# Token-major w_in slices in wider pairs, MLA rotation on GpSimd, and new orders for both mixer stages

## The reference

```
z = rms_norm(h, norm1_g[l]) @ w_in[l]
y = concat([mlstm_mixer(...), mla_mixer(...), gla_mixer(...), conformer_conv(...)])
h = h + group_rms_norm(y, fuse_g[l], 4) @ w_out[l]
u = rms_norm(h, norm2_g[l])
h = h + (swiglu(u, ...) if l == 0 else moe_ffn(u, ...))    # 8 experts, top 2
```

## Time and profile before

| | |
|---|---|
| median of 3 runs | 1340.87 us (1340.64 to 1342.02) |
| the profiled execution's own time | 1339.72 us |
| its span | 1337.5 us |
| TensorE busy | 1259.0 us, 94% of the span |
| VectorE, ScalarE, GpSimd busy | 996.6, 832.9 and 145.0 us |
| mixers of layer 0, from the first transpose to those of the second norm | 17.4 to 154.5 us |
| mixers of layer 1, likewise | 359.7 to 499.1 us |
| mean granted clock of TensorE | 0.972 of full speed |

### The profile page before, as it was taken

One profiled execution on the slowest core, in us unless ns is written; L12 is line 12 of the kernel. 1 busy time (PEld: TensorE's weight loads), 2 busy tenths in 40 slices (PEclk: granted clock), 3 DMA queues, 4 the chain that ended last, 5 costly groups with the idle time before them and its releaser, 6 DMA issues.

```text
span 1337.5 us, 17758 instructions
## 1 busy us (share of the span) xinstructions
PE 1259.0 (94%) x6283; PEld 1053.5 (79%) x6283; DVE 996.6 (75%) x974; ACT 832.9 (62%) x825; POOL 145.0 (11%) x165
## 2 busy tenths in 40 slices
PE   4989899999798986899999999999999999999996
PEld 3889678888697975688888888888888888888885
DVE  4784444444558545888989989989889888988986
ACT  5557534444544744667777677777767767767774
POOL 4647000000045710000000000000000000000000
PEclk9989899999999996999999999999999999999998
DMA  9420685552333048799999999999999999999951
GB/s 292 127 98 8 253 313 189 184 183 75 94 96 126 2 152 304 284 348 331 354 359 341 357 350 340 363 343 349 362 338 358 358 338 357 357 340 354 360 205 49
DMA packets 175056, 347.41 MB, mean 260 GB/s; under 512 B 13166, under 2 KB 54272, under 8 KB 175008
## 3 DMA queue, kind: packets, MB, share of 16 engines
q1 hardware_dynamic: 173744, 344.43, 72.7%
q0 software_dynamic: 1232, 2.33, 0.8%
q10 hardware_dynamic: 32, 0.01, 0.0%
HBM read 345.68 MB, written 1.05 MB: 259 GB/s over the span
## 4 chain that ended last, share of the span: by engine, by line
PE 89%; DVE 6%; ACT 2%; DMA 2%; issue 0%; SPq 0%; DVEq 0%; ACTq 0%
PE bank L1583 15%; PE bank L1585 15%; PE bank L1584 15%; PE bank L1601 8%; PE bank L1600 8%; PE bank L1602 8%; PE bank L1553 3%; PE bank L1554 3%; PE bank L1555 3%; PE bank L1609 2%; PE bank L1943 1%; DVE low L970 1%; DVE uTl L988 1%; PE bank L1529 1%; PE bank L1728 1%; DMA ring<-in_w_in_dram 1%
## 5 line engine op out<-in xcount | busy, mean ns | idle before, releaser
L970 DVE TENSOR_TENSOR low<-ring,high 128x2048 fp32r<-128x2048 f32 x305 | 692.2, 2285 | 149.0 <-ACT high L613 146.8
L613 ACT ACTIVATE high<-ring 128x2048 fp32r<-128x2048 f32 x327 | 624.3, 1912 | 235.6 <-PE bank L1585 151.0
L1583 PE MATMUL bank<-high,uTh 128*128 128x512 f32 x880 | 350.7, 399 | 9.1 <-DVE uTl L988 3.3
L1585 PE MATMUL bank<-high,uTl 128*128 128x512 f32 x880 | 345.9, 393 | 0.0
L1584 PE MATMUL bank<-low,uTh 128*128 128x512 f32 x880 | 345.3, 392 | 0.0
L1583 PEld LDWEIGHTS bank<-high,uTh 128*128 128x128 f32 x880 | 166.8, 189 | 47.1 <-issue 7.1
L1585 PEld LDWEIGHTS bank<-high,uTl 128*128 128x128 f32 x880 | 166.7, 189 | 35.9
L1584 PEld LDWEIGHTS bank<-low,uTh 128*128 128x128 f32 x880 | 167.0, 190 | 32.7
L1601 PE MATMUL bank<-low,moe_hTh 128*128 128x512 f32 x352 | 140.1, 398 | 0.0
L1600 PE MATMUL bank<-high,moe_hTh 128*128 128x512 f32 x352 | 139.3, 396 | 0.0
L1602 PE MATMUL bank<-high,moe_hTl 128*128 128x512 f32 x352 | 138.5, 394 | 0.0
(11 more groups left out here) (370 smaller groups left out, 1483.0 us busy)
## 6 DMA issues: line engine op xcount, KB each, us to landing
ring<-in_moe_w_up_dram SPq DMA_DIRECT2D x176, 512.0 KB, 5.3
ring<-in_moe_w_gate_dram SPq DMA_DIRECT2D x176, 512.0 KB, 5.5
ring<-in_moe_w_down_dram SPq DMA_DIRECT2D x176, 512.0 KB, 5.2
ring<-in_w_in_dram SPq DMA_DIRECT2D x36, 512.0 KB, 4.8
ring<-in_ffn_w_up_dram SPq DMA_DIRECT2D x22, 512.0 KB, 5.2
ring<-in_ffn_w_gate_dram SPq DMA_DIRECT2D x22, 512.0 KB, 7.8
ring<-in_ffn_w_down_dram SPq DMA_DIRECT2D x22, 512.0 KB, 4.1
ring<-in_w_out_dram SPq DMA_DIRECT2D x16, 512.0 KB, 3.7
```

The source lines that it names most:

```text
L613: act.activation(high[:, n % SPLIT, 0:width], slot(n)[:, 0:width], ACT.Copy).then_inc(s["high_ready"], 1)
L970: dve.tensor_tensor(low[:, n % SPLIT, 0:width], slot(n)[:, 0:width], high[:, n % SPLIT, 0:width].bitcast(F32), ALU.subtract).then_inc(s["l ...
L1583: pe.matmul(o, ah, bh, start=(kd == 0), stop=False)
L1585: last = pe.matmul(o, al, bh, start=False, stop=(kd == KD - 1))
```

## The change

The 11 pieces of `w_in` are cut anew. Gates, both latents, the rotary key and the GLA's a (376 columns) are one token-major slice that comes first, as two pieces l0 and l1 of five and three feature blocks. The GLA's v and r (512 columns) become rg0 and rg1, the mLSTM's v and o (512 columns) become vo0 and vo1. Each pair fills one bank of PSUM for each token tile. Three streams of 48 matmuls, 376 or 512 columns wide, thus stand in the place of six of 176 to 256. The first half of l0 waits for each group of `uTl` apart. The rotation is done by GpSimd in eight operations. Two absolute values are taken by ScalarE instead of three small VectorE steps each, VectorE's min and subtract become one step, the four small `gref` steps and `negm` go to ScalarE, and the exponential of minus m is made from a TensorE sum. The rest is order: the small chains of gates and latents come before the convolution on VectorE, `fuse_transposes` 2 and 3 stand at other places among the halves of the output product, and banks are given out anew.

```diff
 W_IN_PIECES = {
-    "b": [(2424, 256)],
-    "a": [(2168, 256)],
-    "kv": [(1224, 160), (2152, 16)],
-    "if": [(1024, 200)],
-    "gqk": [(1384, 256)],
-    "mq": [(0, 256)],
-    "mk": [(256, 256)],
-    "v": [(512, 256)],
-    "o": [(768, 256)],
-    "r": [(1896, 256)],
-    "gv": [(1640, 256)],
+    "l0": ([(1024, 360), (2152, 16)], 0, 5),
+    "l1": ([(1024, 360), (2152, 16)], 5, 8),
+    "b": ([(2424, 256)], 0, 8),
+    "a": ([(2168, 256)], 0, 8),
+    "mq": ([(0, 256)], 0, 8),
+    "mk": ([(256, 256)], 0, 8),
+    "gqk": ([(1384, 256)], 0, 8),
+    "rg0": ([(1640, 512)], 0, 4),
+    "rg1": ([(1640, 512)], 4, 8),
+    "vo0": ([(512, 512)], 0, 4),
+    "vo1": ([(512, 512)], 4, 8),
 }
...
-        FUSE_BANKS = (2, 2, 4, 2)
+        FUSE_BANKS = (5, 0, 0, 0)
...
@@ gpsimd
-                split_low("if")
-                split_low("gqk")
+                split_low("a")
                 split_low("mq")
                 split_low("mk")
...
+                pool.wait_ge(s["kv_out"], l + 1)
+                pool.wait_ge(s["q_out"], l + 1)
...
+                for i, (a, b) in enumerate(((x1, cos), (x2, sin), (x2, cos), (x1, sin))):
+                    chain.done(pool.tensor_tensor(rt[:, i, :, :, :], a, b, ALU.mult))
+                chain.wait()
+                for i, op in ((0, ALU.subtract), (1, ALU.add)):
+                    out_ = slice(64 + 16 * i, 80 + 16 * i)
+                    pool.tensor_tensor(qtok[:, :, :, out_], rt[:, 2 * i, :, 0:4, :], rt[:, 2 * i + 1, :, 0:4, :], op)
+                    last = pool.tensor_tensor(ktok[:, :, :, out_], bc(rt[:, 2 * i, :, 4:5, :], [P, TT, HEADS, 16]),
+                                              bc(rt[:, 2 * i + 1, :, 4:5, :], [P, TT, HEADS, 16]), op)
+                last.then_inc(s["rot_ready"], 1)
...
@@ scalar
+                split_in("vo0")
                 for hd in range(HEADS):
...
                 last.then_inc(s["p_ready"], 1)
-                split_in("gv")
...
@@ tensor
-                pe.wait_ge(s["utl_ready"], 4 * (3 * l + 1))
...
+                        b = PAIR_BANKS[name[:-1]][i]
+                        if k0 == 0:
+                            claim(b, *reader)
+                        for k in range(k0, k1):
+                            if name == "l0" and i == 0 and k % 2 == 0:
+                                pe.wait_ge(s["utl_ready"], 4 * 3 * l + k // 2 + 1)
...
                 out_half(0, 1)
+                out_half(1, 0)
                 fuse_transposes(l, 2)
-                out_half(1, 0)
                 out_half(1, 1)
+                fuse_transposes(l, 3)
                 out_half(2, 0)
-                fuse_transposes(l, 3)
                 out_half(2, 1)
```

More of the change, by code:

```diff
@@ L57, with in_columns, in_width @@
 FEATURE_MAJOR = ("b", "a", "gqk", "mq", "mk")
+PAIR_ENDS = ("l1", "rg1", "vo1")
+def in_columns(name):
+    return sum(w for _, w in W_IN_PIECES[name][0])
+def in_width(name):
+    _, k0, k1 = W_IN_PIECES[name]
+    return (k1 - k0) * in_columns(name)
 POOL_LOWS = (3, 14)
@@ L1145, in gla_gates @@
[L1145 to L1153 removed]
+                dve.wait_ge(s["zl_ready"], 2 * (l + 1))
@@ L1207, in _ @@
-                for t in range(TT):
-                    dve.tensor_copy(qtok[:, t, :, 64:96], rot[:, t, 0:4, :])
-                    last = dve.tensor_copy(ktok[:, t, :, 64:96], bc(rot[:, t, 4:5, :], [P, HEADS, 32]))
-                last.then_inc(s["rot_ready"], 1)
-                dve.wait_ge(s["mcol_tr"], l + 1)
-                dve.tensor_copy(mcol[:, :], bank[0][:, 0:16]).then_inc(s["mcol_ready"], 1)
-                conv_steps(14, 16)
+                conv_steps(0, 8)
+                qk_conv("mq", 0, "qconv_ready")
@@ new lines, in _ @@
+                last.then_inc(s["ckv_tr"], 1)
+                half("b", 1)
+                pe.wait_ge(s["ckv_ready"], l + 1)
+                pe.wait_ge(s["ukv_in"], 64 * (l + 1))
+                claim(7, "gx_ready", l + 1)
+                pe.matmul(bank[7][:, 0:S], walpha[:, :], aT[:, :], start=True, stop=True).then_inc(s["gpre_ready"], 1)
+                pe.wait_ge(s["lf_ready"], l + 1)
+                claim(3, "mcum_ready", l + 1)
+                for t in range(TT):
+                    pe.transpose(bank[3][0:4, t * P:(t + 1) * P], gb[:, t, 0:4], ident[:, :])
+                    last = pe.transpose(bank[3][0:4, S + t * P:S + (t + 1) * P], gb[:, t, 4:8], ident[:, :])
@@ L1740, in _ @@
-                piece("if", "zif_ready")
-                pe.wait_ge(s["zkv_ready"], l + 1)
-                claim(7, "ckv_ready", l + 1)
-                for t in range(TT):
-                    pe.transpose(bank[7][:, t * P:(t + 1) * P], zkv[:, t, 0:P], ident[:, :])
-                    last = pe.transpose(bank[7][0:16, S + t * P:S + (t + 1) * P], zkv[:, t, 160:176], ident[:, :])
-                last.then_inc(s["ckv_tr"], 1)
-                half("gqk", 0, "gqk_ready")
-                pe.wait_ge(s["zif_ready"], l + 1)
@@ L1761, in _ @@
-                pe.matmul(bank[5][:, 0:S], walpha[:, :], aT[:, :], start=True, stop=True).then_inc(s["gpre_ready"], 1)
-                for t in range(TT):
-                    b = (7, 0)[t]
+                for t, b in enumerate(KV_BANKS):
                     claim(b, "kv_out", l + 1)
@@ L1843, in _ @@
                 last.then_inc(s["pv_ready"], 1)
+                pe.wait_ge(s["conv_done"], l + 1)
+                claim(4, "conf_n", l + 1)
+                for t in range(TT):
+                    for c in range(2):
+                        last = pe.transpose(bank[4][:, t * 256 + c * P:t * 256 + (c + 1) * P],
+                                            cacc[:, c, t * P:(t + 1) * P], ident[:, :])
+                last.then_inc(s["conf_tr"], 1)
+                piece("vo1")
+                pe.wait_ge(s["gla_qk"], l + 1)
@@ new lines, in _ @@
+                pe.wait_ge(s["gv_ready"], l + 1)
+                claim(2, "y_g", l + 1)
+                for t in range(TT):
+                    for hd in range(HEADS):
+                        o = bank[2][:, t * 256 + hd * DH:t * 256 + (hd + 1) * DH]
+                        v = gv[:, :, hd * DH:(hd + 1) * DH]
+                        if t == 0:
+                            last = pe.matmul(o, gS[:, hd, 0, :], v[:, 0, :], start=True, stop=True)
+                        else:
+                            pe.matmul(o, gS[:, hd, 1, :], v[:, 0, :], start=True, stop=False)
+                            last = pe.matmul(o, gS[:, hd, 2, :], v[:, 1, :], start=False, stop=True)
```

468 lines of the change are left out of this document (220 added, 248 removed).

## The result

The changed kernel takes 1304.20 us (median of 4 runs, 1299.99 to 1307.55); the kernel before, on the same chip, 1341.03 (4 runs, 1340.64 to 1342.02). The ratio is 0.9723, with a 95% interval of 0.9685 to 0.9761. A second set on another occasion gave 1305.17 against 1340.36, ratio 0.9733 (0.9719 to 0.9748). The profiled execution took 1299.99 us, the fastest of the four, with a span of 1298.0.

The account below looks back on a forecast made before the run. TensorE, busy 94% of the span, was taken as the bound, so gains lay in its time and gaps. Layer 0's 17.1 us and layer 1's 15.7 sum to 32.8: 1308.1 for a median, range 1301 to 1314, 1300 to 1320 with late cases.

Parts of the forecast that it names:

- five signs: No `ktok`/`qtok` wait; 376-column starts every 0.16-0.18 us; `uTl` wait at most 1; rotation 3-5; last fuse transposes at 103-107.
- Wider products: Token-major `w_in` matmuls: 2.55 us less for gates and latents, 1.2 for v, o, r and gv; 3.75 a layer.
- The rotation: Rotated keys in mid mk: GpSimd takes 4.0 us, ready 3.2 early; wait 4.8 and lower clock go, 6.7 a layer.
- vacated VectorE time: VectorE time freed by moving the rotation: costs and gains nothing by itself, since TensorE did not wait for the convolution.
- First group of `uTl`: Each layer's start: TensorE begins after two of eight `uTl` steps, 2.4 us earlier, idle time about 0.6 us.
- the clock behind it: Lower clock after the `uTl` wait costs 1.3 us in all; half its removal counted, 0.65 a layer.
- Start of layer 0: VectorE's copy of the gains stands behind fewer low-part columns: 1.0 us gained, between 0 and 2; nothing in layer 1.
- Output product: End of mixer part: last fuse transposes one half step earlier, 2.7 us a layer; 0.4 more in layer 0.
- New waits: Second fuse transposes wait for bank 0, 0.3 to 0.6 us; with others of that kind, 0.5 lost a layer.
- the rival in ScalarE's queue: vo0's high part amid the softmax's exponentials delays the probabilities' transposes: 5 us a layer, 1318; chance 0.14.
- the late rotation: GpSimd operations of 1.31 us each make TensorE wait 3.3 us, plus lower clock: 5.2 a layer, 1318; chance 0.13.
- the slow GpSimd: Strided, broadcast rotation operands many times slower on GpSimd: at 3.2 us each about 1346, slower than before; chance 0.03.

Follow-up runs that it names:

- second profile: The changed kernel run again unedited, its profiled execution at 1305.92 us with a span of 1304.1.
- e2_narrow: Changed kernel with each 376-column matmul issued as 200 and 176, each 512 as two of 256: median 1320.34 us, profiled execution 1311.55.
- e5_before_rot_pool: Kernel before, with only the rotation moved from VectorE to GpSimd, between the low parts of mk and v: 1326.50 us, ratio 0.9904.
- e6_rot_vector: Changed kernel with the rotation's same eight operations back on VectorE, before piece mq's convolution: 1306.40 us, ratio 0.9745.
- e4_all_groups: Changed kernel with the first l0 matmul waiting again for all four groups of `uTl`: 1310.62 us, ratio 0.9776.
- five variants: Five edited versions of the changed kernel that leave its wait for the first `uTl` group as it is; medians 1301.77 to 1314.13 us.
- e9_cols_early: Changed kernel with VectorE's first copy of the gains ahead of layer 0's normalization, not behind the low parts of l0 and l1: 1301.77 us, ratio 0.9710.
- e3_tail: Changed kernel with the last fuse transposes put back behind one more half of the output product: 1310.10 us, ratio 0.9766.
- e10_h_first: Changed kernel with h added before the first feed-forward piece's low part, and fewer bank claims before layer 0's feed-forward: 1304.26 us, ratio 0.9736.

## Why the prediction held, step by step

1308.1 us was forecast, 1304.2 and 1305.2 are the medians of the two sets: a gain of 32.8 us forecast and of 35.2 to 36.8 measured. All five signs named for "right" are there: no wait for `ktok` or `qtok`, 376 columns every 0.173 us, `uTl` waits of 0.8 and 0.9, a rotation of 3.8, and 103.9 us from the first l0 matmul to the last fuse transposes in both layers of the first profile. The mechanism is right, but the total is closer than its parts, as three stretches show (gain in us, against the kernel before):

| stretch | forecast | first profile | second profile |
|---|---|---|---|
| layer 0, to the first `w_in` matmul | 3.4 | 3.6 | 3.6 |
| layer 0, from there to the last fuse transposes | 13.3 | 15.2 | 14.7 |
| layer 0, from there to h's transposes | 0.4 | -0.1 | -1.6 |
| layer 1, transposes to the first `w_in` matmul | 2.4 | 2.3 | 2.3 |
| layer 1, from there to the last fuse transposes | 13.3 | 14.7 | 13.2 |
| layer 1, from there to h's transposes | 0 | 2.5 | 2.6 |

The long stretches gained up to 1.9 us more than their terms. The last ones missed both ways, and in layer 0 two errors cancel: that its sum came so near is luck. The parts:

- **Layer 0**: 17.1 us forecast, 16.6 and 18.7 in the two profiles. **Layer 1**: 15.7 forecast, 18.1 and 19.5. Most of what the sum missed lies in layer 1.
- **Wider products**, 3.75 a layer. The guessed 0.170 us for 376 columns is 0.173 (9 starts). The Trainium skill (TensorE: Matmul & The Clock Gate, section "Wait — 56ns, not 53.3ns?") gives an estimate of 159 ns there, and the trace does not agree, as at 512. Undoing the widths costs 2.8 to 3.3 us a layer in the trace of e2_narrow: by that trace the term was 0.5 to 0.9 too large, and four slower executions without a trace leave this open. One part of it is plain: in the trace of e2_narrow the 0.4 us wait for bank 0 is absent, so the widths win that much less.
- **The rotation**, 6.7 a layer: 6.7 and 6.8 when it is done alone (e5_before_rot_pool). GpSimd's 3.8 us and its 3.3 us to spare are the 4.0 and 3.2 of the text. What the text did not see is that the engine is not the point in the changed kernel: with everything else in its new order VectorE does it in time too (e6_rot_vector). Where the text said that the vacated VectorE time gains nothing by itself, it was right for TensorE; but with VectorE's queue in its new order and the rotation in eight operations, the wait is gone without GpSimd. How much of this is the order and how much the two operations fewer was not tested.
- **First group of `uTl`**, 2.4, and the clock behind it, counted half, 0.65: e4_all_groups gives 2.3 and 1.0 to 1.5 in layer 0, where the whole dip goes: counting half of it was 0.4 to 0.9 too little. In layer 1 the first l0 matmul to the rotated queries' transposes takes 35.6 us in both profiles of the changed kernel, so none of it is left there; but in five variants 2.1 to 2.4 us of it are, and the text was right to leave this open.
- **Start of layer 0**, 1.0: the first transposes begin 1.35 us earlier (16.03 against 17.38). The cause given, the copy of the gains behind two low parts, is shown by e9_cols_early, which takes 3.9 us more from the same place.
- **Output product**, 2.7 in both: e3_tail gives the 2.8 us wait back in each. In layer 0 that chain and TensorE's own work now end within 1.4 us of each other, as tight as the text's sum made it. In layer 1 more was gained than the step: the wait of 5.5 us fell to 0.3, 5.2 us. This is the term whose size was missed most. The text counted one half step, and took the load's landing as fixed. ScalarE's wait for the first piece of the feed-forward, before and then after:

```profile
493.55 1.91 ACT L613 ACTIVATE high<-ring 128x2048 fp32r<-128x2048 f32 x1 [7.26 <-DMA ring<-in_moe_w_up_dram]
```
```profile
454.79 1.92 ACT L640 ACTIVATE high<-ring 128x2048 fp32r<-128x2048 f32 x1 [4.78 <-DMA ring<-in_moe_w_up_dram]
```

  From the last fuse transposes to the end of that wait it took 8.7 us before (484.81 to 493.55) and 6.3 now (448.53 to 454.79), 6.1 in the second profile: 2.5 us that nobody planned, and with them layer 1 comes to 18.2. This is not the chance of one execution. The same wait is 7.25 us in e5_before_rot_pool, the other trace of the old order:

```profile
479.95 1.91 ACT L628 ACTIVATE high<-ring 128x2048 fp32r<-128x2048 f32 x1 [7.25 <-DMA ring<-in_moe_w_up_dram]
```

  In the twelve traces of the new order it is 4.4 to 4.8, but for the 5.75 of e2_narrow. Which part of the new order makes this load land sooner was not tested. In layer 0 there is no such gain: 4.25 and 4.40 us in the old order, 4.2 to 6.5 from one trace to another in the new, which is scatter.
- **New waits**, 0.5 a layer: 0.4 us for bank 0 in both. No wait before the probabilities' transposes: the rival in ScalarE's queue did not come about, nor did the late rotation. The price of the slow GpSimd, 1346, had a slip: at 3.2 us for each operation and the 1.35 us of the copies the wait is 18.4 us, which makes about 1349. Nothing hung on it.
- **Not foreseen**: the spread. The stretches at the lower clock behind the small matmuls of the attention part come in most profiles (in layer 1 of ten of the twelve in the new order, in layer 0 of five), but in neither layer of the changed kernel's first one nor of e10_h_first. Each is worth 1.7 us and begins right behind the first two decays. The lower clock that in five variants lasts past the start of layer 1 is worth 2.1 to 2.4. What brings either on in one execution and not in another stays open; no idle time stands right ahead of the first kind, and putting half of gqk ahead of the decays did not keep it away.

## What to carry to other kernels

When an operation is late because another engine's operations slow it down, look both ways: moving it to that engine worked, and so did another place in its own engine's queue, in two operations fewer; only an experiment with the rest in its new order tells what is doing the work. At the end of a stage compare the chain over the next load's landing with the compute that covers it. Here they ended within 1.4 us of each other, so the landing's scatter set the time; taking the load's consumer off the path (h before the low part) removed that wait, though no gain could be told in the times. A small copy placed behind long operations is cheap to find in the list of waits: here it brought the first matmul 3.9 us forward. And a term sized from one trace of each kernel can be wrong by the stretches at the lower clock, 1.7 us each: compare the same stretch in several traces before putting a difference down to an edit.

## What the runs showed of the hardware

A matmul of 376 columns in this float32r stream starts every 0.173 us, of 200 and 176 columns every 0.112. GpSimd takes 0.46 us for a sum of 128 x 128 and 0.50 (0.60 in e5_before_rot_pool) for a product of 128 x 160 whose operands are broadcasts and runs of 16 elements; the five products of 128 x 128 in the earlier trace rows took 0.44 each. Four VectorE sums of 128 x 128 took 1.40 to 1.45 us each beside GpSimd and 0.29 alone. The lower granted clock came at 393.6 to 397.0 us of one execution and not of another of the same kernel, with TensorE busy without a gap ahead of it in both; in twelve traces it came 15 times at this place, each time within 1.4 us of the end of the same small matmuls. A first load after an idle stretch made ScalarE wait 7.25 and 7.26 us in the two traces of the old order and 4.4 to 4.8 in eleven of the twelve of the new. And a kernel with narrower matmuls took 1311.6 us once and about 1320 four times; of these one had the same mean granted clock, 0.975, which nothing here explains.
